# Index scores of a sparse-attention block, moved in between the slabs of two projection groups on one Trainium2 core

## The chip, the cores and the metric

The kernel runs on one core of a Trainium2 chip. A core has five engines with their own in-order instruction streams, which meet only through semaphores: TensorE (PE: matmuls into eight PSUM banks), VectorE (DVE), ScalarE (ACT), GpSimd (POOL) and SyncE (SP, which here issues nearly all DMAs). The metric is the device time of one launch in microseconds, lower is better.

## What is computed

One layer of a hybrid block: RMS norm and adaLN, one wide input projection, sparse attention with a light indexer beside a pooling mixer and a recurrent branch, an output projection and an MLP. The change touches the input projection and the indexer:

```python
mod = c_act @ w_mod[l] + b_mod[l]              # 2048 x 12288: six vectors of 2048
h = rms_norm(x, g_pre_mix[l]) * (1.0 + scale1) + shift1
proj = h @ w_in[l]                             # 512 tokens, 2048 features in
q, k, v, q_idx, k_idx, w_idx, pool_in, lru_in, lru_gate = split_columns(proj)
# indexer: 16 heads of 64, in blocks of 128 queries against all 512 keys
dots = jnp.einsum('bqhd,bsd->bqhs', qi, k_idx_f)
score = jnp.einsum('bqh,bqhs->bqs', wi, jax.nn.relu(dots)) * idx_scale
score = jnp.where(admissible, score, -jnp.inf)
_, sel = lax.top_k(score, top_k)               # the attention sees these keys alone
```

All of it is float32. The kernel keeps float32 accuracy by splitting each operand into a high and a low part and adding three matmuls for each product.

## The kernel before

**Slabs.** Weights come in slabs of 2 x 128 rows by 512 columns (512 KB). A slab passes four stages: SP loads it into one of four places of `raw` (`load_slab`), ACT rounds it into `w_hi` (`split`), POOL makes `w_lo = raw - w_hi` (`low`), and PE multiplies it with the 512 tokens (24 matmuls: 4 output tiles x 2 x 3). A projection group of 512 columns is 8 slabs (`SG`). Groups g0 and g1 (keys, key weights, index queries of heads 0 to 7) are slabs 0 to 15; g2 (index queries of heads 8 to 15) is slabs 16 to 23; g3 (recurrent input) is 24 to 31, g4 is 32 to 39, and so on up to slab 95.

**Index scores.** Between g2 and g3 PE computes 64 dots (16 heads x 4 query tiles, three matmuls each, one PSUM bank each) in 16 stages of four banks. ACT takes each through ReLU into one of two buffers of `relu`, DVE multiplies it with the head's weight and adds it to `score`. Each of those steps is 128x512 elements. The keys exist in two copies, in the lower and upper 64 partitions; the second copy is made by two DMAs of SP (`ki_hi[1]`, `ki_lo[1]`).

**Modulation adds.** The vectors of `mod` that are needed later are summed on DVE: 48 slabs of `w_mod` (1 MB each) are loaded by SP into two places (`mod_slab0`, `mod_slab1`), and `mod_add` adds each, scaled, to an accumulator of 128x2048. `mods_beside(s)` is the table that says which of them go with weight slab s: in program order SP issues, for each s, first the modulation slabs of s and then `load_slab(s + 2)`. A modulation slab n may be loaded when adds 0 to n - 2 are done (`mod_step`); a weight slab when POOL is done with the slab four before. DVE runs the adds of s at its own place (`beside_to`). Before the change g2's eight slabs carry 12 adds, the dots another 4 (one after every 16 scores), and slabs 27 to 58 one each.

**What sets the order.** Everything is written out by hand; each engine runs its stream in order. ACT's splits run three slabs ahead of PE. PSUM is used in two halves of four banks, stage by stage (`STAGES`, `begin`): a stage may start when the one two before is read out. `wait_stage`, `act_freed`, `dve_freed` carry this.

Of the kernel before, what the change touches and what calls it, by code (L numbers as in the profile page):

```python
# [22 lines left out]
F32 = mybir.dt.float32  # L23
# [3 lines left out]
ALU = mybir.AluOpType  # L27
# [156 lines left out]
def build(nc, x, x_turned, columns_in, positions, pos_columns, rel_bias, w_mod_first, w_mod, w_in, w_key,  # L184
# [16 lines left out]
    with ExitStack() as ctx:  # L201
# [170 lines left out]
        relu_ready, relu_used, score_done = sem("relu_ready"), sem("relu_used"), sem("score_done")  # L372
        gates_in, pool_in = sem("gates_in"), sem("pool_in")
# [88 lines left out]
        def _(sp):  # L462
# [32 lines left out]
            for s in range(2 * SG - 2, PROJ_SLABS):  # L495
# [187 lines left out]
        def _(pe):  # L683
# [32 lines left out]
            def group(g, stage, emit, act, ready=None, tile=lambda n: n, **how):  # L716
                begin(stage)
                for j in range(SG):
# [7 lines left out]
                    last.then_inc(slab_used, 1)  # L726

# [96 lines left out]
            pe.wait_ge(widx_copied, 1)
            for t in range(TT):
                last = nc.tensor.transpose(bank(n, 0)[:, IH * t:IH * t + IH], widx_t[ID:KW, P * t:P * t + P],
                                           ident[ID:KW, ID:KW])
            last.then_inc(stage_done, 1)
            pe.wait_ge(key_copied, 32)
            for m in range(TT * IH // 4):  # L830
                if m == 0:
# [4 lines left out]
                begin(n)  # L836
# [5 lines left out]
                last.then_inc(stage_done, 1)  # L842
            group(G_LRU, STAGE["g3"], features_out, h)
# [182 lines left out]
        def _(act):  # L1026
# [94 lines left out]
            for g in (1, 2):  # L1121
                s = split_to(s, SG * (g + 1) + 3)
# [6 lines left out]
            for m in range(TT * IH // 4):  # L1129
# [808 lines left out]
```

## Time and profile before

| | us |
|---|---|
| median of three timed runs | 2516.28 |
| lowest, highest | 2509.43, 2518.47 |
| profiled execution, its own time | 2509.14 |
| its span in the trace | 2507.0 |
| granted TensorE clock, mean over the span | 0.98 |

The views used are these: the waits of an engine, the timeline of an engine (start, duration, what it did, idle time before it), the chain that ended last in order of time, and the busy time by stretches. "PE 193.01" below means an instruction that starts 193.01 us after the start of the span. A start of SP is the issue of a DMA. Overlapping PE durations are pipelined matmuls: the distance between two starts tells the pace.

### The profile page before, as it was taken

What the parts mean: (1) busy time and instruction counts of PE and PEld (TensorE: products, weight loads), DVE (VectorE), ACT (ScalarE), POOL (GpSimd) and SP (SyncE); (2) the same over time, 40 slices, a digit from 0 to 9 for tenths busy, and PEclk for the clock granted to TensorE, in tenths of its full rate; (3) what the DMA queues carried; (4) which work ended last, traced back from release to release, by engine and by line L of the source; (5) the groups of instructions that cost most, each with busy time, mean ns of one, the idle gap of its engine ahead of it and who ended that gap; (6) DMA issues with size and microseconds to landing.
All of it is one profiled execution on the core that took longest, in us unless ns stands there. A gap on an engine that the chain in (4) does not pass through costs nothing.

```text
span 2507.0 us, 27318 instructions
## 1 busy us (share of the span) xinstructions
PE 2388.7 (95%) x10722; PEld 1880.6 (75%) x10722; DVE 1213.4 (48%) x1586; ACT 684.5 (27%) x896; POOL 362.5 (14%) x247
## 2 busy tenths in 40 slices
PE   4898899999997999899999999999999999999997
PEld 1456687778776788788888888888888888888885
DVE  5536966699329765643333234343243332333336
ACT  2332624222326422422122122121121221221222
POOL 3543054444427200000000000000000000000000
PEclk8999999989999999999999999999999999999998
DMA  4987266733314276522332332323322333323324
GB/s 180 364 338 272 93 235 235 262 128 95 91 61 129 97 268 244 135 84 93 93 93 94 97 94 92 92 84 100 99 93 92 84 100 95 97 93 92 93 93 168
DMA packets 137504, 340.89 MB, mean 136 GB/s; under 512 B 15824, under 2 KB 17488, under 8 KB 123216
## 3 DMA queue, kind: packets, MB, share of 16 engines
q1 hardware_dynamic: 132208, 331.12, 39.6%
q10 hardware_dynamic: 5216, 8.66, 0.9%
q8 instruction: 55, 0.90, 0.1%
q14 instruction: 25, 0.20, 0.0%
HBM read 322.70 MB, written 16.79 MB: 135 GB/s over the span
## 4 chain that ended last, share of the span: by engine, by line
PE 85%; DVE 7%; DMA 3%; ACT 2%; issue 2%; ACTq 1%; POOL 0%; SPq 0%; DVEq 0%; POOLq 0%
PE psum L694 27%; PE psum L696 27%; PE psum L695 27%; DMA mod_slab<-in_w_mod 2%; DVE acc_a L1394 2%; DMA raw<-in_w_in 1%; PE psum L773 1%; PE psum L758 1%; PE psum L742 1%; PE psum L803 1%; ACT sq_out L1044 0%; DVE pt_lo L1712 0%; PE psum L735 0%; DVE probs L1699 0%; ACTq L1063 0%
## 5 line engine op out<-in xcount | busy, mean ns | idle before, releaser
L1755 DVE TENSOR_TENSOR w_lo<-raw,w_hi 128x1024 fp32r<-128x1024 f32 x256 | 311.7, 1224 | 744.1 <-ACT w_hi L1281 743.7
L694 PE MATMUL psum<-h_hi,w_hi 128*128 128x512 f32 (+1 forms) x1616 | 645.9, 400 | 11.5 <-POOL w_lo L634 5.5
L695 PE MATMUL psum<-h_lo,w_hi 128*128 128x512 f32 (+1 forms) x1616 | 644.6, 399 | 0.0
L696 PE MATMUL psum<-h_hi,w_lo 128*128 128x512 f32 (+1 forms) x1616 | 643.9, 398 | 0.0
L1281 ACT ACTIVATE w_hi<-raw 128x1024 fp32r<-128x1024 f32 x256 | 271.2, 1060 | 1014.9 <-PE psum L696 1005.8
L694 PE MATMUL psum<-w_hi,u_hi 128*128 128x512 f32 x1024 | 408.3, 399 | 0.0
L696 PE MATMUL psum<-w_hi,u_lo 128*128 128x512 f32 x1024 | 403.6, 394 | 0.0
L695 PE MATMUL psum<-w_lo,u_hi 128*128 128x512 f32 x1024 | 401.5, 392 | 0.0
L694 PEld LDWEIGHTS psum<-h_hi,w_hi 128*128 128x128 f32 (+1 forms) x1616 | 306.1, 189 | 91.3 <-issue 9.2
L696 PEld LDWEIGHTS psum<-h_hi,w_lo 128*128 128x128 f32 (+1 forms) x1616 | 306.1, 189 | 75.7 <-issue 0.2
L695 PEld LDWEIGHTS psum<-h_lo,w_hi 128*128 128x128 f32 (+1 forms) x1616 | 306.0, 189 | 74.3 <-issue 0.2
L634 POOL TENSOR_TENSOR w_lo<-raw,w_hi 128x1024 fp32r<-128x1024 f32 (+1 forms) x96 | 240.0, 2505 | 390.4 <-ACT w_hi L1037 390.4
L1037 ACT ACTIVATE w_hi<-raw 128x1024 fp32r<-128x1024 f32 (+1 forms) x128 | 129.2, 1014 | 422.0 <-PE psum L696 285.8
L696 PEld LDWEIGHTS psum<-w_hi,u_lo 128*128 128x128 f32 x1024 | 192.2, 188 | 49.7
L695 PEld LDWEIGHTS psum<-w_lo,u_hi 128*128 128x128 f32 x1024 | 192.2, 188 | 46.3
L694 PEld LDWEIGHTS psum<-w_hi,u_hi 128*128 128x128 f32 x1024 | 192.2, 188 | 44.2 <-DVE w_lo L1755 0.2
L1838 DVE TENSOR_TENSOR y<-y,psum 128x512 f32<-128x512 f32 x112 | 69.5, 683 | 92.0 <-PE psum L696 92.0
L696 PE MATMUL psum<-w_hi,m_lo 128*128 128x512 f32 x256 | 102.5, 400 | 0.0
L694 PE MATMUL psum<-w_hi,m_hi 128*128 128x512 f32 x256 | 101.7, 397 | 0.3 <-issue 0.3
L695 PE MATMUL psum<-w_lo,m_hi 128*128 128x512 f32 x256 | 101.4, 396 | 0.0
L1394 DVE SCALAR_TENSOR_TENSOR acc_a<-mod_slab,c_act,acc_a 128x2048 f32<-128x2048 f32 x30 | 79.3, 2642 | 35.8 <-DMA mod_slab<-in_w_mod 34.8
L1819 DVE TENSOR_TENSOR u_sq<-u_relu 128x512 f32<-128x512 f32 x64 | 44.0, 687 | 64.5 <-ACT u_relu L1327 64.5
(256 smaller groups left out, 2064.1 us busy)
## 6 DMA issues: line engine op xcount, KB each, us to landing
raw<-in_w_mlp_up SPq DMA_DIRECT2D x128, 512.0 KB, 3.7
raw<-in_w_mlp_down SPq DMA_DIRECT2D x128, 512.0 KB, 3.7
mod_slab<-in_w_mod SPq DMA_DIRECT2D x48, 1024.0 KB, 5.9
raw<-in_w_in SPq DMA_DIRECT2D x88, 512.0 KB, 5.9
mod_ring<-in_w_mod_first SPq DMA_DIRECT2D x32, 1024.0 KB, 9.0
raw<-in_w_out SPq DMA_DIRECT2D x32, 512.0 KB, 5.8
slab<-in_w_mod SPq DMA_DIRECT2D x16, 1024.0 KB, 4.9
bias_s<-bias_out ACTq DMA_DIRECT2D x32, 256.0 KB, 6.1
```

The source lines that it names most:

```text
L634: nc.gpsimd.tensor_tensor(w_lo[:, s % RING, :, 0:n], raw[:, s % RING, :, 0:n], w_hi[:, s % RING, :, 0:n].bitcast(F32), ALU.subtract).then_ ...
L694: nc.tensor.matmul(o, a_hi, b_hi, start=first, stop=False)
L695: nc.tensor.matmul(o, a_hi, b_lo, start=False, stop=False)
L696: return nc.tensor.matmul(o, a_lo, b_hi, start=False, stop=last)
L742: last = nc.tensor.matmul(o[:, P * t:P * t + P], src[:, t, P * kt:P * kt + P], diag[:, t, :], start=True, stop=True)
L758: last = nc.tensor.matmul(o[32 * j:32 * j + 32, :], blk_part[:, part, :], steps[:, k % STEP_SLOTS, :], start=part == 0, stop=part == 2)
L1037: nc.scalar.activation(hi, r, ACT.Copy).then_inc(hi_ready, 1)
L1281: nc.scalar.activation(w_hi[:, local % RING, :, :], raw[:, local % RING, :, :], ACT.Copy).then_inc(hi_ready, 1)
L1394: V.scalar_tensor_tensor(acc[:], slab, c_act[:, k:k + 1], acc[:], ALU.mult, ALU.add).then_inc(mod_step, 1)
L1755: V.tensor_tensor(w_lo[:, local % RING, :, :], raw[:, local % RING, :, :], w_hi[:, local % RING, :, :].bitcast(F32), ALU.subtract).then_in ...
L1819: V.tensor_tensor(u_sq[:, b % 2, :], u_relu[:, b % 2, :], u_relu[:, b % 2, :], ALU.mult).then_inc(up_used, 1)
L1838: last = V.tensor_tensor(y, y, bank(n0 + UPG + d, t), ALU.add)
```

## The change

The 64 dots no longer stand as a block between g2 and g3. They are issued as 32 pairs after the slabs of g2 and g3 (`PAIRS_AFTER`: two pairs after each slab, three after the first and second slab of g3, none after the last). The order of the dots goes by heads first, so that the first 16 pairs need the heads 0 to 7 alone. They use banks 4 to 7, one pair on two banks and the next on the other two; g2 and g3 both use banks 0 to 3. A pair waits for the ReLUs of the pair two before. On ACT each split of a slab is followed by that slab's ReLUs, on DVE the modulation adds of a slab by its score adds. The key copies are issued by ACT and not by SP. The 48 modulation adds are spread anew: 24 beside g2 and g3 (two, one, two, one, ...), 24 beside slabs 32 to 55.

```diff
-MOD_DOTS = 3 * SG
-MOD_AGAIN = 3 * SG + 3
+MOD_AGAIN = 4 * SG
+MOD_MORE = 3 * SG
 
 
 def mods_beside(s):
 
-    if 2 * SG <= s < 3 * SG:
+    if 2 * SG <= s < 4 * SG:
         i = s - 2 * SG
         first = MOD_EARLY + 3 * (i // 2) + 2 * (i % 2)
         return [first] if i % 2 else [first, first + 1]
-    if MOD_AGAIN <= s < MOD_AGAIN + 2 * KD:
+    if MOD_AGAIN <= s < MOD_AGAIN + MOD_MORE:
+        return [MOD_EARLY + MOD_MORE + s - MOD_AGAIN]
...
+DOT_PAIRS = TT * IH // 2
+PAIRS_AFTER = (2,) * SG + (3, 3) + (2,) * (SG - 3) + (0,)
+assert sum(PAIRS_AFTER) == DOT_PAIRS and sum(PAIRS_AFTER[:SG]) == DOT_PAIRS // 2
+DOT_BANK = 4
 def dots_of(n):
 
-    pair, n = divmod(n, 2 * IH)
-    return 2 * pair + n % 2, n // 2
+    return n % TT, n // TT
+
+
+def pairs_after(i):
+
+    return range(sum(PAIRS_AFTER[:i]), sum(PAIRS_AFTER[:i + 1]))
+
+
+def dot_bank(k):
+
+    return DOT_BANK + k % 4
...
-                if s == 2 * SG + 2:
-                    sp.wait_ge(idx_ready, 1)
-                    sp.dma_start(ki_hi[1][ID:P, :].bitcast(F32), ki_hi[0][0:ID, :].bitcast(F32)).then_inc(key_copied, 16)
-                    sp.dma_start(ki_lo[1][ID:P, :].bitcast(F32), ki_lo[0][0:ID, :].bitcast(F32)).then_inc(key_copied, 16)
-                if s == MOD_DOTS:
-                    for t in range(TT):
-                        load_mod(DOTS_MOD + t)
...
+            def dots_pair(n):
+                if n == 0:
+                    pe.wait_ge(key_copied, 32)
                     pe.wait_ge(idx_ready, 1 + IH // 4)
-                elif dots_of(4 * m)[1] == IH // 2:
+                elif n == 1:
+                    pe.wait_ge(widx_read, 1)
+                elif n >= 2:
+                    pe.wait_ge(relu_ready, 2 * n - 2)
+                if n == DOT_PAIRS // 2:
                     pe.wait_ge(idx_ready, 1 + IH // 2)
-                n = STAGE[f"dots{m}"]
-                begin(n)
-                for b in range(4):
-                    t, hd = dots_of(4 * m + b)
+                for k in (2 * n, 2 * n + 1):
+                    t, hd = dots_of(k)
                     tok = slice(P * t, P * t + P)
-                    last = three(bank(n, b), qi_hi[:, hd // 2, tok], qi_lo[:, hd // 2, tok], ki_hi[hd % 2][:],
+                    last = three(psum[:, dot_bank(k), :], qi_hi[:, hd // 2, tok], qi_lo[:, hd // 2, tok], ki_hi[hd % 2][:],
                                  ki_lo[hd % 2][:], True, True)
-                last.then_inc(stage_done, 1)
-            group(G_LRU, STAGE["g3"], features_out, h)
+                last.then_inc(dots_done, 1)
+
+            def after_g2(j):
+                if j == 0:
+                    key_weights()
+                for n in pairs_after(j):
+                    dots_pair(n)
+
+            def after_g3(j):
+                for n in pairs_after(SG + j):
+                    dots_pair(n)
+
+            group(G_QI + 1, STAGE["g2"], features_out, h, after=after_g2)
+            group(G_LRU, STAGE["g3"], features_out, h, after=after_g3)
+            pe.wait_ge(relu_ready, 2 * DOT_PAIRS)
...
+            def relus(pairs):
+                for n in pairs:
+                    act.wait_ge(dots_done, n + 1)
+                    for k in (2 * n, 2 * n + 1):
+                        if k >= 2:
+                            act.wait_ge(relu_used, k - 1)
+                        nc.scalar.activation(relu[:, k % 2, :], psum[:, dot_bank(k), :], ACT.Relu).then_inc(relu_ready, 1)
+
+            def index_high(g):
                 done("s1" if g == 1 else "g2")
                 for b in range(4):
                     o = psum[:, QI_BANK + b, :] if g == 1 else bank(STAGE["g2"], b)
                     nc.scalar.activation(qi_hi[:, 4 * (g - 1) + b, :], o, ACT.Copy).then_inc(act_hi, 1)
                 act.wait_ge(act_hi, 1 + 4 * g)
                 act.sem_inc(act_freed, 1)
-            for m in range(TT * IH // 4):
-                done(f"dots{m}")
-                for b in range(4):
-                    k = 4 * m + b
-                    if k >= 2:
-                        act.wait_ge(relu_used, k - 1)
-                    nc.scalar.activation(relu[:, k % 2, :], bank(STAGE[f"dots{m}"], b), ACT.Relu).then_inc(relu_ready, 1)
-                act.wait_ge(relu_ready, 4 * m + 4)
-                act.sem_inc(act_freed, 1)
+
+            act.wait_ge(idx_ready, 1)
+            for part in (ki_hi, ki_lo):
+                act.dma_start(part[1][ID:P, :].bitcast(F32), part[0][0:ID, :].bitcast(F32)).then_inc(key_copied, 16)
+            index_high(1)
+            for j in range(2 * SG):
+                s = split_to(s, 2 * SG + 4 + j)
+                if j == SG - 1:
+                    index_high(2)
+                relus(pairs_after(j))
...
+            def index_low(g):
                 done("s1" if g == 1 else "g2")
                 for b in range(4):
                     k = 4 * (g - 1) + b
                     low(qi_lo[:, k, :], STAGE["s1" if g == 1 else "g2"], b, qi_hi[:, k, :], idx_ready, 2 + k)
                 dve.wait_ge(idx_ready, 1 + 4 * g)
                 dve.sem_inc(dve_freed, 1)
...
+            def add_dots(pairs):
+                for n in pairs:
+                    for k in (2 * n, 2 * n + 1):
+                        t, hd = dots_of(k)
+                        dve.wait_ge(relu_ready, k + 1)
+                        if hd:
+                            dve.wait_ge(relu_used, k - TT + 1)
+                        V.scalar_tensor_tensor(score[:, t, :], relu[:, k % 2, :], w_idx[:, t, hd:hd + 1], score[:, t, :],
+                                               ALU.mult, ALU.add).then_inc(relu_used, 1)
+
+            index_low(1)
+            for t in range(TT):
+                ch.put(V.tensor_scalar(score[:, t, :], pos_k[:], pos_q[:, t:t + 1], NEG, ALU.is_gt, ALU.mult))
             done("widx")
             for t in range(TT):
-                ch.put(V.tensor_scalar(w_idx[:, t, :], bank(STAGE["widx"], 0)[:, IH * t:IH * t + IH], (IH * ID) ** -0.5, None,
+                ch.put(V.tensor_scalar(w_idx[:, t, :], bank(STAGE["widx"], 2)[:, IH * t:IH * t + IH], (IH * ID) ** -0.5, None,
                                        ALU.mult))
-            free()
-
-            for k in range(TT * IH):
-                t, hd = dots_of(k)
-                if k % (2 * IH) == 0:
-                    for u in (t, t + 1):
-                        ch.put(V.tensor_scalar(score[:, u, :], pos_k[:], pos_q[:, u:u + 1], NEG, ALU.is_gt, ALU.mult))
-                    ch.wait()
-                dve.wait_ge(relu_ready, k + 1)
-                if hd:
-                    dve.wait_ge(relu_used, k - 1)
-                V.scalar_tensor_tensor(score[:, t, :], relu[:, k % 2, :], w_idx[:, t, hd:hd + 1], score[:, t, :], ALU.mult,
-                                       ALU.add).then_inc(relu_used, 1)
-                if k % IH == IH - 1:
-                    mod_add(DOTS_MOD + k // IH)
+            ch.wait()
+            dve.sem_inc(widx_read, 1)
+            for j in range(2 * SG):
+                s = beside_to(s, 2 * SG + j + 1)
+                if j == SG - 1:
+                    index_low(2)
+                add_dots(pairs_after(j))
```

The index splits of g2 (`index_high(2)`, `index_low(2)`) must be done before g3 may begin, since g3 uses g2's banks.

**ACT, from the index queries of g1 on.** `w_hi<-raw` is the split of a weight slab, `raw_landed3` the DMA of slab 19. Before:

```order
L1126 ACTIVATE qi_hi<-psum 128x512 [waits widx_copied,act_hi,slab_used]
L1126 ACTIVATE qi_hi<-psum 128x512 x3
L1037 ACTIVATE w_hi<-raw 128x1024 [waits act_hi,slab_used,raw_landed3]
L1037 ACTIVATE w_hi<-raw 128x1024 [waits slab_used,raw_landed0]
L1037 ACTIVATE w_hi<-raw 128x1024 [waits slab_used,raw_landed1]
L1037 ACTIVATE w_hi<-raw 128x1024 [waits slab_used,raw_landed2]
```

Now, the same place:

```order
L1061 ACTIVATE w_hi<-raw 128x1024 [waits act_hi,slab_used,raw_landed3]
L1151 ACTIVATE relu<-psum 128x512 [waits dots_done]
L1151 ACTIVATE relu<-psum 128x512
L1151 ACTIVATE relu<-psum 128x512 [waits relu_used,dots_done]
L1151 ACTIVATE relu<-psum 128x512 [waits relu_used]
L1061 ACTIVATE w_hi<-raw 128x1024 [waits slab_used,raw_landed0]
L1151 ACTIVATE relu<-psum 128x512 [waits relu_used,dots_done]
L1151 ACTIVATE relu<-psum 128x512 [waits relu_used]
```

The splits of slabs 19, 20, ... stood in a row of eight; now four ReLUs stand behind each.

**DVE, from the index queries' low part on.** `acc_a<-mod_slab` is a modulation add, `score<-relu` a score add. Before:

```order
L1547 TENSOR_TENSOR qi_lo<-psum,qi_hi 128x512 [waits act_hi] x3
L1391 TENSOR_SCALAR acc_a<-mod_slab0,c_act 128x2048 [waits idx_ready,mod_landed0]
L1394 SCALAR_TENSOR_TENSOR acc_a<-mod_slab1,c_act,acc_a 128x2048 [waits mod_step,mod_landed1]
L1394 SCALAR_TENSOR_TENSOR acc_a<-mod_slab0,c_act,acc_a 128x2048 [waits mod_step,mod_landed0]
L1394 SCALAR_TENSOR_TENSOR acc_a<-mod_slab1,c_act,acc_a 128x2048 [waits mod_step,mod_landed1]
L1394 SCALAR_TENSOR_TENSOR acc_a<-mod_slab0,c_act,acc_a 128x2048 [waits mod_step,mod_landed0]
```

Now:

```order
L1613 TENSOR_SCALAR w_idx<-psum 128x16 [waits stage_done]
L1613 TENSOR_SCALAR w_idx<-psum 128x16 x3
L1421 TENSOR_SCALAR acc_a<-mod_slab0,c_act 128x2048 [waits dve_chain,mod_landed0]
L1424 SCALAR_TENSOR_TENSOR acc_a<-mod_slab1,c_act,acc_a 128x2048 [waits mod_step,mod_landed1]
L1605 SCALAR_TENSOR_TENSOR score<-relu,w_idx,score 128x512 [waits relu_ready] x4
L1424 SCALAR_TENSOR_TENSOR acc_a<-mod_slab0,c_act,acc_a 128x2048 [waits mod_step,mod_landed0]
L1605 SCALAR_TENSOR_TENSOR score<-relu,w_idx,score 128x512 [waits relu_used,relu_ready] x4
L1424 SCALAR_TENSOR_TENSOR acc_a<-mod_slab1,c_act,acc_a 128x2048 [waits mod_step,mod_landed1]
```

The modulation adds ran one behind the other; now four score adds, which wait for ReLUs, stand between them, and the first add stands behind the key weights, which PE turns after slab 16.

**SP, the loads of slabs 19 to 21 and of what is loaded between them.** Now (the same rows stood there before, with the two key copies behind the second of them):

```order
L491 DMA mod_slab0<-in_w_mod 128x2048 [waits mod_step]
L480 DMA raw<-in_w_in 128x2x512 [waits lo_pool]
L491 DMA mod_slab1<-in_w_mod 128x2048 [waits mod_step]
L491 DMA mod_slab0<-in_w_mod 128x2048 [waits mod_step]
L480 DMA raw<-in_w_in 128x2x512 [waits lo_pool]
L491 DMA mod_slab1<-in_w_mod 128x2048 [waits mod_step]
L480 DMA raw<-in_w_in 128x2x512 [waits lo_pool]
```

Each weight slab is issued behind one or two modulation slabs, and these wait for DVE's adds (`mod_step`). This pattern went on for slabs 18 to 25 and goes on for slabs 18 to 33 now.

## Rows read from the trace of the kernel before

**Rows 1.** Busy time of each engine from g2 to the end of g3, with granted clock.

```profile
core 0: us, PE busy (x) PEld busy (x) DVE busy (x) ACT busy (x) POOL busy (x), PEclk, DMA share, GB/s
193.00:348.00 155.00, 140.53 (x580) 109.69 (x581) 114.69 (x104) 57.00 (x85) 45.60 (x16) 0.97 0.62 228
```

**Rows 2.** Waits of PE, 175 to 300 and 430 to 620 us.

```profile
PE psum L694 <- DVEq L1567: 7.5, 1, 7.5
PE psum L694 <- ACTq L1137: 6.9, 3, 2.9
...
PE psum L694 <- POOL w_lo L634: 5.5, 2, 3.8
```

**Rows 3.** Timeline of PE: start, duration; the first matmuls of g2, and mod2 behind g3.

```profile
193.01 0.66 PE L694 MATMUL psum<-h_hi,w_hi 128*128 128x512 f32 x1 [3.26 <-issue]
...
196.46 0.43 PE L696 MATMUL psum<-h_hi,w_lo 128*128 128x512 f32 x1
...
303.14 0.50 PE L694 MATMUL psum<-h_hi,w_hi 128*128 128x512 f32 x1
...
348.22 3.63 PE L735 MATMUL psum<-ones,acc_a 128*128 128x1 f32 x32
```

**Rows 4.** Timeline of DVE: first modulation add, key weights, score adds.

```profile
195.70 1.29 DVE L1391 TENSOR_SCALAR acc_a<-mod_slab,c_act 128x2048 f32<-128x2048 f32 x1
...
247.52 0.42 DVE L1570 TENSOR_SCALAR w_idx<-psum 128x16 f32<-128x16 f32 x4
...
252.97 11.59 DVE L1583 SCALAR_TENSOR_TENSOR score<-relu,w_idx,score 128x512 f32<-128x512 f32 x16 [4.00 <-ACT relu L1135]
...
304.14 2.83 DVE L1583 SCALAR_TENSOR_TENSOR score<-relu,w_idx,score 128x512 f32<-128x512 f32 x4 [0.31 <-ACT relu L1135]
```

**Rows 5.** Timeline of ACT: splits, index queries and ReLUs, with the idle time before.

```profile
203.13 1.06 ACT L1037 ACTIVATE w_hi<-raw 128x1024 fp32r<-128x1024 f32 x1 [9.93 <-DMA raw<-in_w_in]
212.63 1.06 ACT L1037 ACTIVATE w_hi<-raw 128x1024 fp32r<-128x1024 f32 x1 [8.44 <-DMA raw<-in_w_in]
...
244.20 2.04 ACT L1126 ACTIVATE qi_hi<-psum 128x512 fp32r<-128x512 f32 x4
252.27 1.08 ACT L1135 ACTIVATE relu<-psum 128x512 f32<-128x512 f32 x2 [6.03 <-PE psum L696]
```

**Rows 6.** Timeline of SP: issues of modulation slabs (L478) and weight slabs (L467).

```profile
197.01 0.33 SPq L478 DMA_DIRECT2D mod_slab<-in_w_mod  x1
197.39 0.43 SPq L467 DMA_DIRECT2D raw<-in_w_in  x1
...
204.54 0.43 SPq L467 DMA_DIRECT2D raw<-in_w_in  x1
```

**Rows 7.** Chain that ended last, in order of time: an add, the loads behind it, the split.

```profile
445.79 4.21 DVE acc_a L1394
...
450.01 0.34 SPq L478
...
450.39 5.78 DMA raw<-in_w_in
...
456.20 1.06 ACT w_hi L1037
```

**Rows 8.** Timelines of POOL (a low part) and DVE (adds of the convolution).

```profile
351.92 2.40 POOL L634 TENSOR_TENSOR w_lo<-raw,w_hi 128x1024 fp32r<-128x1024 f32 x1 [4.32 <-ACT w_hi L1037]
...
351.27 4.38 DVE L1599 SCALAR_TENSOR_TENSOR xc<-lru_in,col,xc 128x511 f32<-128x511 f32 x3
...
356.27 2.33 DVE L1599 SCALAR_TENSOR_TENSOR xc<-lru_in,col,xc 128x511 f32<-128x511 f32 x3
```

**Rows 9.** Timeline of DVE from g3 to the sums of the recurrent branch.

```profile
350.69 0.55 DVE L1596 TENSOR_SCALAR xc<-lru_in,col 128x512 f32<-128x512 f32 x1 [5.35 <-ACTq L1150]
...
368.67 0.17 DVE L1473 TENSOR_TENSOR mod<-psum,col 128x16 f32<-128x16 f32 x1
...
401.11 2.35 DVE L1394 SCALAR_TENSOR_TENSOR acc_b<-mod_slab,c_act,acc_b 128x2048 f32<-128x2048 f32 x1 [2.69 <-DMA mod_slab<-in_w_mod]
```

More of the change, by code:

```diff
@@ L90, in mods_beside @@
         return [first] if i % 2 else [first, first + 1]
-    if MOD_AGAIN <= s < MOD_AGAIN + 2 * KD:
-        return [MOD_EARLY + KD + s - MOD_AGAIN]
+    if MOD_AGAIN <= s < MOD_AGAIN + MOD_MORE:
+        return [MOD_EARLY + MOD_MORE + s - MOD_AGAIN]
     return []
-DOTS_MOD = MOD_EARLY + 3 * SG // 2
 STAGES = (
-    [("s0", "AD"), ("s1", "AD"), ("g2", "AD"), ("widx", "D")]
-    + [(f"dots{n}", "A") for n in range(TT * IH // 4)]
[1 row of a table added]
     + [("g3", "A"), ("mod2", "D"), ("g4", "A"), ("rgate", "A"), ("igate", "A"), ("mod3", "D"), ("g5", "A"), ("g6", "A"),
@@ L714, in tokens_out, with group @@
                 return last
-            def group(g, stage, emit, act, ready=None, tile=lambda n: n, **how):
+            def group(g, stage, emit, act, ready=None, tile=lambda n: n, after=lambda j: None, **how):
                 begin(stage)
@@ L726, in group @@
                     last.then_inc(slab_used, 1)
+                    after(j)
             def mod_sum(j):
@@ L820, in _, with key_weights @@
             h = (h_hi, h_lo)
-            group(G_QI + 1, STAGE["g2"], features_out, h)
-            n = STAGE["widx"]
-            begin(n)
[L824 to L827, printed above, removed]
-            last.then_inc(stage_done, 1)
-            pe.wait_ge(key_copied, 32)
-            for m in range(TT * IH // 4):
-                if m == 0:
-                    pe.wait_ge(idx_ready, 1 + IH // 4)
-                elif dots_of(4 * m)[1] == IH // 2:
+            def key_weights():
+                n = STAGE["widx"]
+                begin(n)
+                pe.wait_ge(widx_copied, 1)
+                for t in range(TT):
+                    last = nc.tensor.transpose(bank(n, 2)[:, IH * t:IH * t + IH], widx_t[ID:KW, P * t:P * t + P],
+                                               ident[ID:KW, ID:KW])
+                last.then_inc(stage_done, 1)
@@ L1559, in _ @@
             dve.sem_inc(dve_freed, 1)
-            for g in (1, 2):
-                s = beside_to(s, SG * (g + 1) + (3 if g == 2 else 0))
+            def index_low(g):
                 done("s1" if g == 1 else "g2")
@@ L1567, in _ @@
                 dve.sem_inc(dve_freed, 1)
+            def add_dots(pairs):
[8 more added lines that the diff above has]
+            index_low(1)
+            for t in range(TT):
+                ch.put(V.tensor_scalar(score[:, t, :], pos_k[:], pos_q[:, t:t + 1], NEG, ALU.is_gt, ALU.mult))
             done("widx")
             for t in range(TT):
-                ch.put(V.tensor_scalar(w_idx[:, t, :], bank(STAGE["widx"], 0)[:, IH * t:IH * t + IH], (IH * ID) ** -0.5, None,
+                ch.put(V.tensor_scalar(w_idx[:, t, :], bank(STAGE["widx"], 2)[:, IH * t:IH * t + IH], (IH * ID) ** -0.5, None,
                                        ALU.mult))
-            free()
-            for k in range(TT * IH):
-                t, hd = dots_of(k)
-                if k % (2 * IH) == 0:
-                    for u in (t, t + 1):
-                        ch.put(V.tensor_scalar(score[:, u, :], pos_k[:], pos_q[:, u:u + 1], NEG, ALU.is_gt, ALU.mult))
-                    ch.wait()
-                dve.wait_ge(relu_ready, k + 1)
-                if hd:
-                    dve.wait_ge(relu_used, k - 1)
-                V.scalar_tensor_tensor(score[:, t, :], relu[:, k % 2, :], w_idx[:, t, hd:hd + 1], score[:, t, :], ALU.mult,
-                                       ALU.add).then_inc(relu_used, 1)
-                if k % IH == IH - 1:
-                    mod_add(DOTS_MOD + k // IH)
+            ch.wait()
[5 more added lines that the diff above has]
+                add_dots(pairs_after(j))
             dve.wait_ge(relu_used, TT * IH)
```

10 lines of the change are left out of this document (2 added, 8 removed), and 1 row of the table STAGES.

## The prediction

> **What bounds the kernel now.** I read the busy time of the stretch from g2 to the end of g3 first, then PE's waits, then the timelines of the other engines there. From 193.0 to 348 PE is busy for 140.5 of 155.0 us [rows 1]. Its idle time is 14.4 us in four waits: 7.5 us before the first dot, for the index queries' split, and 6.9 us in three waits inside the block of dots [rows 2]. So PE sets the end, and the most that a better order can win here is those waits and what they cost in clock. PE's own pace: g3 takes from 303.14 to 348.22 for eight slabs, 5.64 us a slab or 0.235 us a matmul; behind an idle of 3.26 us the first eight matmuls of g2 stand 0.43 us apart (193.01 to 196.46), half the pace [rows 3].
>
> **What the change does on PE.** Its matmuls are the same: 16 slabs and 64 dots. One step j (slab 16 + j and its two pairs of dots) needs 5.64 us and 12 matmuls of 0.235, 8.5 us in all. Were nothing else late, the stretch would be shorter by the 14.4 us of waits and by the slow start behind the 7.5 us wait (8 matmuls at 0.43 for 0.235, 1.6 us), some 16 us. DVE has 3.5 us of modulation adds (1.5 of 2.35, the duration in [rows 9]) and 2.85 of score adds a step, ACT 1.06 + 4 x 0.6 [rows 4, 5]: by busy time all fit into 8.5 us.
>
> **What the change does in the order.** It closes a ring of in-order streams, and this is where I expect the time to go. Follow it from the moment A(j - 1) at which DVE ends the score adds of step j - 1. Only then does DVE reach the first modulation add of step j. SP has the next modulation slab waiting for just this add, and the weight slab 19 + j queued behind that modulation slab. ACT has the split of slab 19 + j ahead of the ReLUs of step j, and waits there for the slab's DMA, although PE does not need that slab for two steps. DVE's score adds of step j wait for those ReLUs. In the kernel before, the same loads hung on the same adds, but DVE ran the adds freely and no ReLU stood behind a split until all eight of g2 were done.
>
> The ring's length, term by term:
> - modulation add: 2.35 us [rows 9].
> - from the add's end to the start of the split: the two issues and the landing of 1 MB and 512 KB. Issue at 197.01, split at 203.13, 6.1 us [rows 5, 6]; in the chain of waits 450.01 to 456.20, 6.2 us, again directly behind an add [rows 7]. I take 6.2. Both have little ahead of them in the queue, as here, where a step loads 2 MB. The other end is the slab issued at 204.54 behind two modulation slabs and split at 212.63, 8.1 us [rows 5, 6].
> - split: 1.06 us [rows 5].
> - from the split's end to the first score add: at least one ReLU and a hop, 0.7 us (ACT starts at 252.27, DVE at 252.97) [rows 4, 5]. But POOL starts `low` of the same slab just then, 2.40 us. No row of before has a score add beside a `low`. The nearest is the convolution, the same operation with two inputs of 128 x 512 in SBUF: three take 2.33 us alone and 4.38 us where a `low` (351.92, 2.40) starts beside them [rows 8]. That is almost the whole `low`, so the adds wait until it is over: 2.5 us. The ends are 0.7 and 2.5; I take 2.5, since operation and shape are the same.
> - four score adds: 2.83 us [rows 4], with a hop 2.85.
>
> The sum is 2.35 + 6.2 + 1.06 + 2.5 + 2.85 = 15.0 us a step, against PE's 8.5. PE may issue the dots of a step when the ReLUs of the step before are done, so it is held to the same 15.0.
>
> The Trainium skill bears on the fourth term ("SBUF — State Buffer", Who interferes with whom): a VectorE instruction with two inputs in SBUF contends with a GpSimd one that reads SBUF, and the second to come is blocked until the first is done. The trace agrees for the convolution; for the score adds no run here shows it yet. By it the ring takes 15.0 us, without it 13.2.
>
> **The sum.** Slab 16 ends at 193.0 + 8 x 0.43 + 16 x 0.235 = 200.2. PE turns the key weights (some 0.4 us, four of the small matmuls of mod2, 32 of which take 3.63 [rows 3]), DVE copies them (0.42) and does the first add (1.29) [rows 4]: 202.5. Loads 6.2, split 1.06, 2.5, adds 2.85: A(0) = 215.1. Step 14 is the last with dots. Fourteen rings are 210.0. Steps 8 and 9 have three pairs: 2 x 2 x 0.72 (11.59 us for 16 adds [rows 4]) = 2.9. Step 7 has the index queries of g2 between its split and its ReLUs: 2.04 us of copies on ACT [rows 5], DVE's low part behind them, adds 3.2 instead of 2.5 us after the split, 0.7 more. A(14) = 428.7. The last ReLU is one add earlier, and PE waits for it before mod2: 428.0, where it was 348.2 [rows 3]. That is **+79.8 us**.
>
> Costed at nothing: the key copies on ACT's queue. They delay the index queries of g1 by some 3 us on ACT and DVE, and both then wait for slab 16 and slab 19 anyway. If the copies land late, PE waits at the first pair, which ends long before slab 19 is split; without that cover they would cost their delay once, below 3 us. The wait of g3 for g2's banks lies inside the ring of step 7. What PE loses in clock behind its idle times (1.6 us each) lies inside its slack of 6.5 us a step.
>
> Behind mod2: the copy of g3 and slab 32 follow as before. Four modulation adds now stand between the last score add and the convolution, some 14 us with their loads, so the convolution (350.69 to 368.67, 18 us [rows 9]) starts some 11 us behind slab 32, where it started 1 us ahead of it. Slab 39's load hangs on the add behind the convolution: 442.5 + 18 + 2.35 + 6.2 + 1.06 + 2.4 = 472.5, and PE wants it at 431.7 + 7 x 5.64 = 471.2. That costs 1 to 3 us, and the recurrent branch behind it perhaps as much again. Against it stands that the adds end at slab 55 and not 58: the longer of the two later waits for POOL, 5.5 us together [rows 2], may go. I take 0, with -4 to +6 as bounds.
>
> So the profiled execution would take 2509.1 + 80 = 2589 us, of which 2507.0 is its span and 2.1 lies around it. That execution is 7 us below the median of the three runs (2516.3), so in terms of the median I forecast 2516 + 80 = **2596 us**.
>
> **Rivals.**
> - *The score adds run beside POOL.* For it: no row has the pair. The ring is 13.2 us, 15 x 1.8 = 27 us less: +53, 2569 us. Chance 0.17.
> - *The loads take longer.* A step issues three transfers in 15 us, against it; the 8.1 us row for it. 15 x 1.9 = 28 us more: 2625 us. Chance 0.07.
> - *PE stays at half clock.* With 8.5 us of work in 15 it idles twice a step. In before, it went to half pace behind 3.26 us of idle and was back after 3.5 us of work [rows 3]; at half pace throughout, a step takes 36 x 0.43 = 15.5 us, more than the ring, and PE sets the pace: +7 or so, 2604 us. Speaking for it, the Trainium skill ("TensorE: Matmul & The Clock Gate", HAM oscillation) says that a wait for data that recurs in every tile puts the clock down again in every tile. Against it: after each wait PE has a whole slab of unbroken work. Chance 0.08.
> - *Faster.* The loads stay ahead, and the ring never closes. It would need slab 19 + j to have landed when ACT comes to it, thus a ring below PE's 8.5 us; the landing and the two adds' terms alone are 6.2 + 2.35 + 2.85 = 11.4. Then the 16 us of waits go: 2500 us. Chance 0.04.
> - *The ring closes, but costs 10 to 45 us,* because some term overlaps with another in a way that I don't see. Chance 0.06.
>
> My own case has 0.58: 2596, by itself 2584 to 2610. The range of 8 in 10 takes in the first and the third rival: 2563 to 2620. A measurement of this kernel can tell about 0.5% (13 us) from no change: faster 0.04, same 0.03, slower 0.93.
>
> **What would show it.** Right: in the stretch of g2 and g3 ACT's splits each wait some 5 us or more for the DMA of their slab, and start 15.0 us apart (19.. to 30); score adds come in bursts of four behind the end of a `low`; PE waits for ReLUs twice in most steps; DMA share near one half; mod2 near 428. A split distance near 13 with adds inside the `low` shows the first rival, 8.5 with PE without waits the fast one. Granted clock near 0.5 in whole slabs shows the third. I would be wrong from the ground up if ReLUs of step j started before the split of slab 19 + j.

## The result: slower, and the profile after

| | before | after |
|---|---|---|
| median, us | 2517.38 (4 runs, 2509.43 to 2522.38) | 2584.50 (4 runs, 2583.01 to 2586.42) |
| profiled execution, span, us | 2507.0 | 2580.9 |
| mean granted clock over the span | 0.98 | 0.97 |

The ratio is 1.027, 95% interval 1.0242 to 1.0298: 2.7% slower, 67 us. The forecast was 2596 us, with a range of 2563 to 2620. The two profiled executions differ by 73.9 us of span. Their line numbers differ too: a split of a weight slab is now L1061, a ReLU L1151, a score add L1605, a modulation add L1424, `low` L640, SP's weight slab L480 and its modulation slab L491.

Busy time of each engine from g2 to shortly before mod2, as in [rows 1]; the number in brackets counts instructions:

```profile
core 0: us, PE busy (x) PEld busy (x) DVE busy (x) ACT busy (x) POOL busy (x), PEclk, DMA share, GB/s
193.00:418.00 225.00, 167.06 (x580) 124.14 (x580) 122.48 (x99) 51.62 (x82) 33.12 (x14) 0.82 0.37 138
```

The same 580 matmul records that took a stretch of 155 us now take 225. The DMA share fell from 0.62 to 0.37 and POOL did fewer slabs in a longer time. Nobody is full: TensorE, the busiest, works for 74% of the stretch. It waits instead, and the longest times for ReLUs. Waits of PE from 175 to 660 us, as in [rows 2]:

```profile
PE psum L700 <- ACT relu L1151: 46.9, 22, 4.7
PE psum L700 <- issue: 13.8, 2, 10.6
PE psum L742 <- ACT relu L1151: 7.3, 1, 7.3
PE psum L700 <- POOL w_lo L640: 3.6, 1, 3.6
PE psum L876 <- ACTq L1177: 1.3, 1, 1.3
```

The 10.6 us stand before g3 (316.62), whose banks DVE's low part of the index queries left at 316.46; as predicted they lie inside step 7 of the ring. Waits for a ReLU, up to two a step, make a sum, not a cause: ACT's stream says what the ReLUs wait for. Timeline of ACT, as in [rows 5] (start, duration, what it did, idle time before it and its releaser):

```profile
209.70 1.06 ACT L1061 ACTIVATE w_hi<-raw 128x1024 fp32r<-128x1024 f32 x1 [13.69 <-DMA raw<-in_w_in]
210.66 1.06 ACT L1151 ACTIVATE relu<-psum 128x512 f32<-128x512 f32 x2
213.85 1.20 ACT L1151 ACTIVATE relu<-psum 128x512 f32<-128x512 f32 x2 [2.12 <-DVE score L1605]
224.33 1.06 ACT L1061 ACTIVATE w_hi<-raw 128x1024 fp32r<-128x1024 f32 x1 [9.28 <-DMA raw<-in_w_in]
...
238.96 1.06 ACT L1061 ACTIVATE w_hi<-raw 128x1024 fp32r<-128x1024 f32 x1 [9.30 <-DMA raw<-in_w_in]
```

Each split comes after more than 9 us of idle that a slab's DMA ended, and the ReLUs run directly behind it. The distance is 14.63 us. The DMA itself is late because DVE's modulation add is. Timelines of DVE, of POOL and of SP over the same steps, as in [rows 4, 8] and [rows 6]:

```profile
211.28 4.62 DVE L1605 SCALAR_TENSOR_TENSOR score<-relu,w_idx,score 128x512 f32<-128x512 f32 x4 [5.29 <-ACT relu L1151]
215.81 2.35 DVE L1424 SCALAR_TENSOR_TENSOR acc_a<-mod_slab,c_act,acc_a 128x2048 f32<-128x2048 f32 x1
225.90 4.61 DVE L1605 SCALAR_TENSOR_TENSOR score<-relu,w_idx,score 128x512 f32<-128x512 f32 x4 [7.74 <-ACT relu L1151]
230.42 4.80 DVE L1424 SCALAR_TENSOR_TENSOR acc_a<-mod_slab,c_act,acc_a 128x2048 f32<-128x2048 f32 x2
```

```profile
210.83 2.37 POOL L640 TENSOR_TENSOR w_lo<-raw,w_hi 128x1024 fp32r<-128x1024 f32 x1 [21.04 <-ACT w_hi L1061]
225.46 2.36 POOL L640 TENSOR_TENSOR w_lo<-raw,w_hi 128x1024 fp32r<-128x1024 f32 x1 [12.25 <-ACT w_hi L1061]
```

```profile
206.01 12.50 SPq L491 DMA_DIRECT2D mod_slab<-in_w_mod  x2
218.56 0.43 SPq L480 DMA_DIRECT2D raw<-in_w_in  x1
```

This is the ring, once around: DVE's add ends at 218.16, SP issues the modulation slab (the second of the two in the row of 206.01, which ends at 218.51) and then the weight slab (218.56), ACT splits it at 224.33, POOL and DVE follow at 225.46 and 225.90, the four score adds end at 230.51, and only then does DVE reach the next add (230.42 in the records, which overlap by 0.09).

### The profile page after: what moved, and what is told of

The parts are those of the page before. It is cut to its first block, busy times and chain, and to the rows that moved or that the text cites. A ratio compares the mean times of both kernels' runs of the same rounds, so it can differ in the third digit from the quotient of the medians.

```text
span 2580.9 us, 27301 instructions
## 1 busy us (share of the span) xinstructions
PE 2411.7 (93%) x10722; PEld 1892.8 (73%) x10722; DVE 1225.5 (47%) x1586; ACT 681.3 (26%) x896; POOL 352.9 (14%) x247
## 4 chain that ended last, share of the span: by engine, by line
PE 79%; DVE 10%; DMA 4%; ACT 2%; issue 2%; ACTq 1%; POOL 0%; SPq 0%; DVEq 0%; POOLq 0%
PE psum L700 25%; PE psum L702 25%; PE psum L701 25%; DMA raw<-in_w_in 3%; DVE score L1605 2%; DVE acc_a L1424 1%; DMA mod_slab<-in_w_mod 1%; DVE acc_b L1424 1%; PE psum L780 1%; ACT relu L1151 1%; PE psum L765 1%; PE psum L749 1%; PE psum L810 1%; DVE steps L1458 1%; DVE xc L1634 1%
## 5 line engine op out<-in xcount | busy, mean ns | idle before, releaser
L640 POOL TENSOR_TENSOR w_lo<-raw,w_hi 128x1024 fp32r<-128x1024 f32 (+1 forms) x96 | 230.9, 2409 | 473.8 <-ACT w_hi L1061 473.8
L1061 ACT ACTIVATE w_hi<-raw 128x1024 fp32r<-128x1024 f32 (+1 forms) x128 | 129.3, 1014 | 503.0 <-PE psum L702 270.8
L1605 DVE SCALAR_TENSOR_TENSOR score<-relu,w_idx,score 128x512 f32<-128x512 f32 x64 | 69.3, 1123 | 92.4 <-ACT relu L1151 91.3
L1424 DVE SCALAR_TENSOR_TENSOR acc_a<-mod_slab,c_act,acc_a 128x2048 f32<-128x2048 f32 x30 | 75.8, 2525 | 22.4 <-DMA mod_slab<-in_w_mod 20.9
```

The lines of the kernel that those rows point to most:

```text
L640: nc.gpsimd.tensor_tensor(w_lo[:, s % RING, :, 0:n], raw[:, s % RING, :, 0:n], w_hi[:, s % RING, :, 0:n].bitcast(F32), ALU.subtract).then_ ...
L1061: nc.scalar.activation(hi, r, ACT.Copy).then_inc(hi_ready, 1)
L1424: V.scalar_tensor_tensor(acc[:], slab, c_act[:, k:k + 1], acc[:], ALU.mult, ALU.add).then_inc(mod_step, 1)
L1605: V.scalar_tensor_tensor(score[:, t, :], relu[:, k % 2, :], w_idx[:, t, hd:hd + 1], score[:, t, :], ALU.mult, ALU.add).then_inc(relu_used, 1)
```

## The experiments

The theory is the ring of the prediction: three in-order streams (DVE, SP, ACT), each with one item ahead of another that it need not precede. If it is right, turning round a single pair on a single engine opens it; if it is not (TensorE at half clock, VectorE or GpSimd too full, the key copies), such an edit changes little. The kernel before took 2512.71 us (median of 14 runs) beside the first four experiments and 2513.53 us (17 runs) beside the last four; all ratios are to these.

**ACT: ReLUs ahead of the split.**

```diff
             for j in range(2 * SG):
-                s = split_to(s, 2 * SG + 4 + j)
                 if j == SG - 1:
                     index_high(2)
                 relus(pairs_after(j))
+                s = split_to(s, 2 * SG + 4 + j)
```

> The changed kernel with one thing swapped on ScalarE: in each step the ReLUs of slab 16 + j now stand ahead of the split of slab 19 + j. Theory (ring): the loss comes from the ring of modulation add, loads queued behind it, split, ReLUs, score adds. The swap takes the split and the load out of it; the longest chain of a step is then TensorE's own 8.5 us, mod2 starts near 332 us for 424.8, and the time falls by 75 to 93 us, to 2495 to 2510, below the kernel before. Rival (TensorE's pace): if the many short idle times and the low clock of TensorE held the step, the order on ScalarE would change little: above 2570.

Measured: 2493.58 us, ratio 0.9928 (0.9908 to 0.9948). The timeline of PE has mod2 at

```profile
335.95 4.91 PE L742 MATMUL psum<-ones,acc_a 128*128 128x1 f32 x32
```

That is 88.8 us earlier than after the change, in an execution whose g2 began 5.7 us later. No wait for a ReLU is left in PE's list up to 620 us. The split ahead of the ReLUs is what held them. The median lies 1.4 us below the range that was expected.

**SP: the weight slab ahead of the modulation slabs.**

```diff
             for s in range(2 * SG - 2, PROJ_SLABS):
+                load_slab(s + 2)
                 for g in mods_beside(s):
                     load_mod(g)
-                load_slab(s + 2)
```

> The changed kernel with one thing swapped on SyncE: for each s the weight slab s + 2 is issued ahead of the modulation slabs of s, ScalarE's order is as changed. Theory (ring): the weight slab no longer waits for the modulation add of its own step but for one of the step before, so it has landed when ScalarE comes to its split; mod2 near 332 us, 2495 to 2510. Rival (ScalarE's order alone is to blame, whatever the loads): no gain, above 2570. Rival (more transfers in flight collide): splits still wait for their DMA, between 2520 and 2570.

Measured: 2488.77 us, ratio 0.9915 (0.9889 to 0.9941). Busy time by stretch, and mod2 on PE:

```profile
193.00:330.00 137.00, 135.49 (x577) 108.84 (x577) 123.92 (x104) 57.23 (x88) 52.83 (x16) 0.99 0.65 238
```

```profile
330.74 4.50 PE L742 MATMUL psum<-ones,acc_a 128*128 128x1 f32 x32
```

PE is busy for 135.5 of 137 us at a granted clock of 0.99. mod2 starts where it was expected, 94.0 us earlier than after the change and 17.5 us earlier than before it; the median is 6 us better than the range that was expected. ACT's timeline of this kernel still has a wait for the DMA, but a short one, and ReLUs on both sides of each split:

```profile
209.06 1.06 ACT L1061 ACTIVATE w_hi<-raw 128x1024 fp32r<-128x1024 f32 x1 [1.79 <-DMA raw<-in_w_in]
...
217.69 1.06 ACT L1061 ACTIVATE w_hi<-raw 128x1024 fp32r<-128x1024 f32 x1 [3.19 <-DMA raw<-in_w_in]
```

**Both cuts together.** The diff is the sum of the two above.

> The changed kernel with both cuts of the ring: ScalarE takes the scores' relus ahead of the split, and SyncE the slab's load ahead of the dots' two. Theory (one closed ring, so that either cut opens it and TensorE's own work is the pace after one): no gain over either, 2486 to 2494, with the next dots from 330 to 336 us. Rival (each cut takes away its own delay, and the two add up): below 2480.

Measured: 2488.48 us, ratio 0.9909 (0.988 to 0.9938), with mod2 at

```profile
329.44 3.73 PE L742 MATMUL psum<-ones,acc_a 128*128 128x1 f32 x32
```

mod2 and the median lie beside those of SP's swap alone, and the ratio cannot be told from either cut's: there was one ring and not two delays that add up. After one cut TensorE's own work sets the pace, and the second edit works on something that is hidden.

**SP's swap in the kernel before.** The same two lines are exchanged there, the dots stay a block.

> The kernel before with SyncE's order alone swapped: a slab's load ahead of the next dots' modulation slabs; the score dots stay in their three blocks. Theory (what the swap is worth in the changed kernel is the ring that it opens, and the kernel before has no ring to open, since no split there waits on a score add): TensorE's waits around the dots stay at 7.5 and 5.5 us, and at most the waits for w_lo behind the scan go: 2507 to 2513. Rival (the swapped order is itself the gain, whatever the order of the dots): about 2490.

Measured: 2508.14 us, ratio 0.998 (0.9961 to 0.9999). PE's waits from 185 to 620 us:

```profile
PE psum L694 <- DVEq L1567: 9.6, 1, 9.6
PE psum L694 <- ACTq L1137: 7.0, 4, 2.9
PE psum L694 <- issue: 3.3, 1, 3.3
PE psum L694 <- POOL w_lo L634: 3.2, 1, 3.2
```

The waits around the block of dots are all there (9.6 and 7.0 us, 7.5 and 6.9 in [rows 2]); only those for POOL are 2.3 us shorter in sum. The swap by itself is worth 5.4 us, at the edge of what can be told. So most of the 24 us that lie between the kernel before and the changed kernel with SP's swap are not the swap's own: it is the scores between the slabs that give them, and the swap that lets them.

**A smaller modulation add in the closed ring.** In 22 of the 24 modulation slabs beside the dots only the first 1024 of 2048 columns are loaded and added.

```diff
+                w = D if k == 0 or g >= MOD_EARLY + MOD_MORE else D // 2
-                sp.dma_start(dst, w_mod_d[:, k, D * m:D * (m + 1)]).then_inc(mod_landed[slot], 16)
+                sp.dma_start(dst[:, 0:w], w_mod_d[:, k, D * m:D * m + w]).then_inc(mod_landed[slot], 16)
...
-                    V.scalar_tensor_tensor(acc[:], slab, c_act[:, k:k + 1], acc[:], ALU.mult, ALU.add).then_inc(mod_step, 1)
+                    w = D if g >= MOD_EARLY + MOD_MORE else D // 2
+                    V.scalar_tensor_tensor(acc[:, 0:w], slab[:, 0:w], c_act[:, k:k + 1], acc[:, 0:w], ALU.mult, ALU.add).then_inc(mod_step, 1)
```

> The changed kernel with the ring left closed, where 22 of the 24 modulation slabs beside the dots are loaded and added in their first half alone (half of the columns of those sums are left out). The modulation add falls from 2.35 to about 1.25 us, and the two loads of a step carry half a modulation slab less. Theory (the ring is the sum of its terms): a step of 14.6 us becomes 12.1, 14 steps 35 us, and the time about 2550. Rival (the step is set by VectorE's or GpSimd's own load, or by TensorE at half clock): the distance between splits stays above 14 us and the time above 2575.

Measured: 2553.99 us, ratio 1.0156 (1.0127 to 1.0185). Timelines of DVE, ACT and PE (the window of the last ends at 400 us, so its row has 18 of mod2's 32 matmuls):

```profile
217.38 1.28 DVE L1426 SCALAR_TENSOR_TENSOR acc_a<-mod_slab,c_act,acc_a 128x1024 f32<-128x1024 f32 x1
```

```profile
223.59 1.06 ACT L1062 ACTIVATE w_hi<-raw 128x1024 fp32r<-128x1024 f32 x1 [6.98 <-DMA raw<-in_w_in]
...
235.94 1.06 ACT L1062 ACTIVATE w_hi<-raw 128x1024 fp32r<-128x1024 f32 x1 [7.01 <-DMA raw<-in_w_in]
```

```profile
396.24 4.00 PE L743 MATMUL psum<-ones,acc_a 128*128 128x1 f32 x18 [4.99 <-ACT relu L1152]
```

The add is 1.07 us shorter, the way from its end to the split 4.93 us instead of 6.17, and the distance of the splits is 12.35 us instead of 14.63: the two terms went down by 2.31, the ring by 2.28. Fourteen rings are 32 us; mod2 comes 28.5 us earlier in an execution in which g2 began 3.1 us later. A ring whose length is the sum of its terms does this. An engine that is too full would have given less: POOL's and ACT's work was untouched, and DVE's own fell by 1.6 us a step (1.5 adds), less than the 2.28.

**POOL's `low` behind the score adds.** It takes away the collision of `low` with the four score adds, and leaves the ring closed.

```diff
                 pool.wait_ge(hi_ready, s + 1)
+                if 2 * SG + 3 <= s < 4 * SG + 2:
+                    pool.wait_ge(relu_used, 2 * sum(PAIRS_AFTER[:s - 2 * SG - 2]))
```

> The changed kernel, but GpSimd starts the low part of slab 19 + j only when the score adds of step j are done, so that the two never overlap. If the adds are really held up by it, four adds take 2.85 us for 4.6, a ring takes 12.8 us for 14.6, fifteen rings save 26 us: 2558, mod2 near 399. If the long adds had another cause (the ReLUs or the banks), no change: 2584.

Measured: 2565.55 us, ratio 1.021 (1.0169 to 1.0251). Timelines of DVE, POOL and ACT:

```profile
211.78 2.90 DVE L1607 SCALAR_TENSOR_TENSOR score<-relu,w_idx,score 128x512 f32<-128x512 f32 x4 [5.23 <-ACT relu L1153]
...
224.64 2.89 DVE L1607 SCALAR_TENSOR_TENSOR score<-relu,w_idx,score 128x512 f32<-128x512 f32 x4 [7.70 <-ACT relu L1153]
227.45 6.75 DVE L1426 SCALAR_TENSOR_TENSOR acc_a<-mod_slab,c_act,acc_a 128x2048 f32<-128x2048 f32 x2
```

```profile
227.67 4.38 POOL L642 TENSOR_TENSOR w_lo<-raw,w_hi 128x1024 fp32r<-128x1024 f32 x1 [8.48 <-DVE score L1607]
```

```profile
210.21 1.06 ACT L1063 ACTIVATE w_hi<-raw 128x1024 fp32r<-128x1024 f32 x1 [12.51 <-DMA raw<-in_w_in]
...
223.07 1.06 ACT L1063 ACTIVATE w_hi<-raw 128x1024 fp32r<-128x1024 f32 x1 [9.23 <-DMA raw<-in_w_in]
```

The four score adds are back at 2.90 us, the ring is 12.97 us in the mean of three (12.86, 13.21, 12.83), near the 13.2 that the first rival of the prediction gave it, and mod2 starts 23.0 us earlier (401.78), in an execution in which g2 began 1.7 us later. So the hold-up by `low` is a term of the ring and was worth 1.7 us in each. The collision has only moved: `low` now starts beside a modulation add and takes 4.4 us, and where a second modulation add follows, that add is held in its turn (6.75 us for two, not 4.80). The median is 19 us below that of the changed kernel, but 7.6 us above the expected 2558: in the profiled executions, 13.4 us apart, some 10 of the 23 us were given back behind mod2. PE waited 3.5 us before the gates there, for 1.3, and behind mod2 some 28 more matmuls stand at half pace, at 0.195 us each 5.5 us; why the clock fell more often there stays open.

**The key copies back on SP's queue,** behind the load of slab 18.

```diff
+                if s == 2 * SG:
+                    sp.wait_ge(idx_ready, 1)
+                    for part in (ki_hi, ki_lo):
+                        sp.dma_start(part[1][ID:P, :].bitcast(F32), part[0][0:ID, :].bitcast(F32)).then_inc(key_copied, 16)
...
-            act.wait_ge(idx_ready, 1)
-            for part in (ki_hi, ki_lo):
-                act.dma_start(part[1][ID:P, :].bitcast(F32), part[0][0:ID, :].bitcast(F32)).then_inc(key_copied, 16)
             index_high(1)
```

> The changed kernel with the two key copies back on SyncE's queue, behind the load of slab 18. They were costed at nothing, since both ScalarE and VectorE wait for slab 16 and slab 19 anyway: within 3 us of the changed kernel, 2581 to 2588, with mod2 within 2 us of 424.8.

Measured: 2584.76 us (one run), mod2 at 425.65 for 424.78. This part of the change costs nothing that one run can show.

**A later wait: two splits moved ahead of the scan's end.** With the ring open by SP's swap, PE's longest wait was 4.85 us for `w_lo` of slab 45 (PE has done 120 matmuls, five slabs, since slab 40; the expectation calls it 46), whose split stood on ACT behind the wait for the recurrent scan. On top of SP's swap:

```diff
-            s = split_to(s, SG * 5 + 5)
+            s = split_to(s, SG * 5 + 6)
             ch.link(nc.scalar.activation(lru_in[:], r_t[:], ACT.Sqrt, scale=-0.25))
             act.sem_inc(branch_act, 1)
+            s = split_to(s, SG * 5 + 7)
             act.wait_ge(branch_dve, SCANNED)
```

> The kernel with SyncE's half of the loop swapped (a slab's load ahead of the dots' two) and, beside it, ScalarE's splits of slabs 45 and 46 put around the square root of the scan's end instead of behind the wait for it. In the kernel without this second edit TensorE waited 4.85 us for w_lo of slab 46 and ran at half clock for a stretch behind it. Theory (the late split alone is what that wait is made of): the wait goes, with some 1 to 2 us of half clock behind it, and the time falls from 2488.8 to about 2482. Rival (the slab's load or GpSimd's low half comes last there): the wait stays at over 2 us and the time within 2 us of 2489.

Measured: 2490.11 us (6 runs, 2482.41 to 2491.84), ratio 0.9901 (0.988 to 0.9923). PE's waits from 185 to 620 us:

```profile
PE psum L700 <- issue: 5.0, 2, 3.3
PE psum L876 <- ACTq L1177: 2.7, 1, 2.7
PE psum L700 <- POOL w_lo L640: 2.4, 1, 2.4
```

PE's timelines have the wait for `w_lo` with SP's swap alone, and now, at

```profile
426.45 0.79 PE L700 MATMUL psum<-h_hi,w_hi 128*128 128x512 f32 x1 [4.85 <-POOL w_lo L640]
```

```profile
460.21 0.79 PE L700 MATMUL psum<-h_hi,w_hi 128*128 128x512 f32 x1 [2.38 <-POOL w_lo L640]
```

These are not the same wait. Between slab 40 and 460.21 PE has done 264 matmuls, eleven slabs, without a wait: the one before slab 45 is gone, as the theory said, and the one of 2.4 us is before slab 51, whose split (455.32 on ACT) stands behind the copy of g5, which waits for DVE. The kernel with the ReLUs ahead of the split, without this edit, has that wait too (2.48 us at 467.91). The 2.7 us before the gates lie ahead of the edit in ACT's stream. So the late split made the 4.85 us, but the time did not follow: the median is not the theory's 2482 but within the 2 us of 2489 that the rival named, and the ratio cannot be told from that of SP's swap alone (0.9915). Whether the early splits are worth anything stays open.

## Why the prediction was right, step by step

**The ring.** Right in mechanism, place and nearly in size: 14.63 us for a predicted 15.0. By its terms, from the step that ends at 230.51:

| term | predicted | measured |
|---|---|---|
| modulation add | 2.35 | 2.35, less 0.09 of overlap with the score adds |
| add's end to split | 6.2 | 6.17 (218.16 to 224.33) |
| split | 1.06 | 1.06 |
| split's end to `low`'s end | 2.5 | 2.43 (225.39 to 227.82) |
| four score adds from there | 2.85 | 2.69 (to 230.51) |
| sum | 15.0 | 14.6 |

I was too long by 0.07 us up to the end of `low`, 0.16 in the four adds and 0.09 at the seam to the next add. `low` starts 0.07 us behind the split and holds the adds from there, and I had allowed more for the hops.

**The score adds beside `low`.** This was the term without a row of its own, bounded by 0.7 and 2.5 us, and I took 2.5 from the convolution. The four adds take 4.62 us with a `low` that starts 0.45 us ahead of them, 2.90 without one (POOL's `low` behind the score adds). That matches the end of `low` plus four adds of 0.67. ACT saw the same: its third ReLU, which needs the buffer that the first add frees, waited 2.11 us for it (to 228.46, 0.64 us behind the end of `low`), and 0.39 us where `low` came later. The rule of the Trainium skill ("SBUF — State Buffer", Who interferes with whom), that the second to come is blocked until the first is done, agrees with these rows in both directions: in the experiment it is `low` that came second, and it took 4.4 us instead of 2.4.

**The start and the end of the ring.** DVE's first burst of score adds ended at 215.90, predicted 215.1; the last at 425.58, predicted 428.7. Between them lie 209.7 us where I had 213.6. Fourteen rings of 14.63 are 204.8. Of the remaining 4.9 (predicted 3.6) the three-pair steps took the 2.9 that I gave them and step 7 1.1 for 0.7; two other distances were longer by 0.3 and 0.7 us, the second where a weight slab took 6.83 us from the add's end to its split. The start was 0.8 us late, which is what PE lost by doing twelve and not eight matmuls of slab 16 at half pace. The key copies delayed the index queries of g1 by 2.8 us, as in the timeline of ACT (193.94, where it was 191.13), and DVE's low parts with them, but the key weights, the first work of the ring on DVE, waited for PE and not for that:

```profile
192.72 0.53 ACTq L1163 DMA_DIRECT2D ki_hi<-ki_hi  x1
193.29 0.61 ACTq L1163 DMA_DIRECT2D ki_lo<-ki_lo  x1
193.94 2.06 ACT L1157 ACTIVATE qi_hi<-psum 128x512 fp32r<-128x512 f32 x4 [3.12 <-issue]
```

```profile
201.65 0.42 DVE L1613 TENSOR_SCALAR w_idx<-psum 128x16 f32<-128x16 f32 x4 [2.70 <-PE psum L834]
```

**Behind mod2.** The sum here was 0 with −4 to +6, and the true −2.7 (from +76.6 to +73.9) is made of two larger things that I didn't see. That they nearly cancel is luck. The start of a few pieces of work on PE's timeline, in us:

| | before | after | difference |
|---|---|---|---|
| mod2 | 348.2 | 424.8 | +76.6 |
| slab 32 | 351.7 | 431.6 | +79.9 |
| gates of the recurrent branch | 396.8 | 479.3 | +82.5 |
| slab 40 | 407.2 | 491.7 | +84.5 |
| mod4 | 552.5 | 633.6 | +81.1 |
| first product of keys and queries | 753.1 | 828.4 | +75.3 |
| output projection | 842.5 | 916.5 | +74.0 |
| end of the span | 2507.0 | 2580.9 | +73.9 |

First, up to slab 40, 7.9 us are added, mostly clock. PE's timeline, as in [rows 3]:

```profile
424.78 6.98 PE L742 MATMUL psum<-ones,acc_a 128*128 128x1 f32 x32 [7.31 <-ACT relu L1151]
431.63 0.77 PE L700 MATMUL psum<-h_hi,w_hi 128*128 128x512 f32 x1
432.20 0.63 PE L701 MATMUL psum<-h_lo,w_hi 128*128 128x512 f32 x1
```

Behind 7.31 us of idle the 32 small matmuls take 6.98 us for 3.63, and twelve matmuls of slab 32 stand 0.43 us apart for 0.235, at a granted clock of 0.50 (1.2 of 2.4 GHz): 3.3 and 2.3 us. The wait before the gates is 1.3 us; about 1 us of the 7.9 is not placed. Second, from slab 40 on, 10.6 us come back. The kernel before has 51 matmuls at half pace there (runs that start at 522, 557, 703, 754, 796 and 982 us), the changed one 15 (560 and 1056): 36 times 0.195 is 7.0 us. mod4's small matmuls took 4.58 us and now 3.63, 1.0 us. The waits for `w_lo` are 5.5 us and now 3.6. These 9.9 us leave 0.7 unexplained. Before slab 59 PE waited 3.81 us (521.54) and now not at all: the longer of the two waits is gone, as the prediction said it might be with the adds ending at slab 55. The one before slab 51 grew from 1.70 to 3.56 us. Which idle times put the clock down I read from the two traces alone; no experiment was made on it.

The stall of slab 39, 1 to 3 us in the prediction, didn't come. The supplying side was right: the convolution ran from 441.13 and its successor, the modulation add, started at 459.75; slab 39 was then split and its low part ready at 471.81 (predicted 472.5):

```profile
441.13 0.54 DVE L1631 TENSOR_SCALAR xc<-lru_in,col 128x512 f32<-128x512 f32 x1
...
459.75 2.35 DVE L1424 SCALAR_TENSOR_TENSOR acc_b<-mod_slab,c_act,acc_b 128x2048 f32<-128x2048 f32 x1 [0.22 <-DVE mod L1506]
```

```profile
469.42 2.39 POOL L640 TENSOR_TENSOR w_lo<-raw,w_hi 128x1024 fp32r<-128x1024 f32 x1 [14.01 <-ACT w_hi L1061]
```

PE reached the slab only at 473.7 (5.64 us ahead of the gates at 479.3), since it had lost 5.6 us at half clock. The prediction had it there at 471.2. The margin was 2 us; that this term came to nothing is luck, too.

**The rivals.** *Score adds beside POOL*: false, the adds were held; with `low` behind the adds the ring came to 12.97 us, near the 13.2 that I had given this rival. *Loads take longer*: 6.17 us, false. *PE at half clock*: the granted clock was indeed 0.82 in the stretch (0.97 before), so this cost existed, but it lay in the slack of each step: in the execution with half modulation adds the ring shortened by its own terms with nothing done for the clock. The Trainium skill ("TensorE: Matmul & The Clock Gate", HAM oscillation) has the clock fall again at each wait that recurs; the trace agrees in the main, with that 0.82 and with half-pace matmuls in 12 places between 226 and 411 us. The loss was hidden here because the ring, and not PE, set the pace. *Faster*: the 16 us that I said PE would win were it alone are real, 17.5 us at mod2 with SP's swap; it needs the ring open.

**The sum against the median.** +80 was predicted, +73.9 measured between the profiled executions, but +67 between the medians: the kernel before happened to be profiled 8 us below its median, the changed one 1.5 us. Of the error of 11.5 us, 6.1 are the ring and what came behind mod2, 6.8 this choice of executions, and 1.4 went the other way, since the median before is 2517.4 and not 2516. The 2584.5 lies at the very edge of the 2584 to 2610 that I gave my own case: the mechanism and the step fit better than that number.

## What to carry to other kernels

When work is moved in between the items of a prefetching loop, write down for each in-order stream which item now stands ahead of which, and look for a closed way round: here add, load, split, ReLU, score add, add. Its length is the sum of latencies, landing of the DMA included, and it becomes the pace however idle every engine is. To open it, turn round one pair on one engine, the item that is needed later behind the one that is needed now; a second cut brought nothing here, and the first turned 2.7% slower into 0.85% faster (2488.77 us, the scores between the slabs with SP's weight slab ahead of the modulation slabs). DVE's pair was not turned round, and a third place for the modulation slabs, another way that might loosen the ring, was not tried.

## What the runs showed of the hardware

- A VectorE add with two inputs in SBUF that meets a GpSimd `low` is held until the `low` is over: 4.62 us for four score adds instead of 2.90, and the other way round `low` takes 4.4 us for 2.4. Delaying one of the two by a wait shifts the collision to the next operation (6.75 us for two modulation adds, 4.80 alone).
- Small matmuls (128x1) pay nearly the whole clock: 6.98 us for 32 behind 7.31 us of idle (granted clock 0.50), 3.63 in the kernel before (granted clock 1.00).
- 1 MB and 512 KB in a row took 6.17 us from the end of the add that released them to the split, 512 KB and 512 KB 4.93 us. Half a megabyte less saved 1.24 us.
